# One weight tile's low half, made by VectorE alone or by VectorE and GpSimd in halves, in a hybrid decoder block

## The reference, cut to what matters

```python
h = concat(meta_tokens[16], x)                       # 272 rows of 1024
u = rms_norm(h, norm1_w)
proj = u @ w_in                                      # attention q,k,v | deltanet q,k,v | gates, beta, decay
y_a = differential_attention(a_q, a_k, a_v, ...)     # two softmax maps per head, 8 heads, blocks of 128 queries
y_d = gated_deltanet(d_q, d_k, d_v, d_gate, ...)     # causal convolution of 4 taps + SiLU, then a chunked delta rule
mixed = sigmoid(gate_a) * (y_a @ w_branch_attn) + sigmoid(gate_d) * (y_d @ w_branch_dn)
h = h + mixed @ w_out
h = h + hierarchical_moe(rms_norm(h, norm2_w), ...)  # 32 experts, top 1 group, top 2 experts in it
out = rms_norm(h, final_norm_w)[16:]
```

## Time and profile before

| what | value |
| --- | --- |
| median of 3 runs | 670.09 us (669.33 to 672.49) |
| the profiled execution | 666.38 us, of which the span from the first to the last instruction is 664.5 us |
| busy share of the span | PE 91%, PEld 76%, DVE 49%, ACT 40%, POOL 8% |
| mean granted TensorE clock | 0.969 |
| bytes read from HBM | 154 MB, 233 GB/s over the span |

### The profile page before, as it was taken

How to read it: one execution, slowest core, us unless ns; L and a number is a source line. 1 busy time by engine, 2 the same in 40 slices (tenths; PEclk the granted TensorE clock), 3 DMA queues, 4 the chain that set the end, 5 groups by cost and what they waited for, 6 DMA issues and landing times.

```text
span 664.5 us, 14325 instructions
## 1 busy us (share of the span) xinstructions
PE 603.1 (91%) x5931; PEld 505.1 (76%) x5931; DVE 327.3 (49%) x693; ACT 268.8 (40%) x598; POOL 55.2 (8%) x102
## 2 busy tenths in 40 slices
PE   8999999899987998999999999999999788687874
PEld 8999989788987888999899999997554443334451
DVE  5344376888876768465757478624112110111112
ACT  6245567676769445323532665413110010000003
POOL 8300011111000001100310120000000000000000
PEclk9799999999999999999999999999999977887999
DMA  9744543243335323221223259999999999999994
GB/s 290 237 158 161 177 141 106 86 128 127 128 127 190 124 68 128 66 66 64 65 66 114 79 174 341 419 420 419 421 364 421 419 424 421 424 421 423 419 409 160
DMA packets 68560, 156.04 MB, mean 235 GB/s; under 512 B 4818, under 2 KB 54116, under 8 KB 56596
## 3 DMA queue, kind: packets, MB, share of 16 engines
q1 hardware_dynamic: 67136, 154.89, 61.5%
q0 software_dynamic: 176, 0.17, 0.2%
q10 hardware_dynamic: 1188, 0.12, 0.2%
HBM read 154.12 MB, written 1.05 MB: 233 GB/s over the span
## 4 chain that ended last, share of the span: by engine, by line
PE 63%; DMA 10%; SPq 8%; ACT 8%; DVE 6%; issue 3%; ACTq 0%; DVEq 0%
PE bank L840 32%; DMA arena<-in_expert_w_gate_dram 8%; PE bank L1251 6%; SPq L511 6%; PE bank L1027 5%; PE bank L825 3%; SPq L606 2%; DMA arena<-in_expert_w_down_dram 2%; PE bank L1005 2%; PE bank L1232 2%; DVE ring_lo L329 1%; PE bank L1276 1%; ACT w_hi L324 1%; PE bank L1287 1%; PE bank L908 1%
## 5 line engine op out<-in xcount | busy, mean ns | idle before, releaser
L840 PE MATMUL bank<-uT_hi,w_hi 128*128 128x272 f32 (+1 forms) x568 | 169.0, 297 | 6.5 <-issue 4.9
L840 PE MATMUL bank<-uT_lo,w_hi 128*128 128x272 f32 (+1 forms) x568 | 162.9, 287 | 0.0
L840 PE MATMUL bank<-uT_hi,ring_lo 128*128 128x272 f32 (+1 forms) x568 | 162.6, 286 | 0.0
L329 DVE TENSOR_TENSOR ring_lo<-arena,w_hi 128x1024 fp32r<-128x1024 f32 x88 | 108.8, 1238 | 48.2 <-ACT w_hi L324 48.1
L840 PEld LDWEIGHTS bank<-uT_hi,w_hi 128*128 128x128 f32 x568 | 107.9, 190 | 11.5 <-issue 9.9
L840 PEld LDWEIGHTS bank<-uT_lo,w_hi 128*128 128x128 f32 x568 | 107.8, 190 | 0.5 <-issue 0.5
L840 PEld LDWEIGHTS bank<-uT_hi,ring_lo 128*128 128x128 f32 x568 | 108.0, 190 | 0.0
L324 ACT ACTIVATE w_hi<-arena 128x1024 fp32r<-128x1024 f32 x88 | 91.8, 1051 | 0.7 <-DMA arena<-in_w_in_dram 0.5
L1251 PE MATMUL bank<-arena 128*32 128x256 f32 x1024 | 64.8, 410 | 19.1 <-DMA arena<-in_expert_w_gate_dram 19.1
L1251 PEld LDWEIGHTS bank<-arena 128*32 128x32 f32 x1024 | 35.1, 118 | 43.8 <-issue 23.8
L1896 DVE SCALAR_TENSOR_TENSOR arena<-arena 128x272 f32<-128x272 f32 x72 | 35.9, 499 | 19.4 <-ACT arena L1413 18.9
(11 more groups left out here) (367 smaller groups left out, 1031.9 us busy)
## 6 DMA issues: line engine op xcount, KB each, us to landing
arena<-in_w_in_dram SPq DMA_DIRECT2D x36, 1024.0 KB, 5.0
arena<-in_expert_w_gate_dram SPq DMA_DIRECT2D x32, 1024.0 KB, 26.0
arena<-in_expert_w_up_dram SPq DMA_DIRECT2D x32, 1024.0 KB, 22.1
arena<-in_expert_w_down_dram SPq DMA_DIRECT2D x29, 1024.0 KB, 22.0
arena<-in_w_branch_attn_dram SPq DMA_DIRECT2D x4, 1024.0 KB, 5.2
arena<-in_w_branch_dn_dram SPq DMA_DIRECT2D x4, 1024.0 KB, 5.3
arena<-in_w_out_dram SPq DMA_DIRECT2D x4, 1024.0 KB, 8.5
arena<-in_expert_w_down_dram SPq DMA_DIRECT2D x6, 512.0 KB, 18.7
```

The source lines that it names most:

```text
L329: nc.vector.tensor_tensor(low_of(SPLIT[q]), src, w_hi[q % NSPLIT].bitcast(F32), ALU.subtract).then_inc(w_lo_ready, 1)
L840: last = pe.matmul(ps[:, 0:b.shape[2]], a[:, c, :], b[:, c, :], start=(c == 0 and i == 0), stop=(c == NC - 1 and i == 2))
```

## The change

In the slots the low part of a tile is made by two engines. For the tiles in `SHARED`, 24 to 47 (all of dq, dk and dv), VectorE's `split_low` now covers chunks 0 to 3 alone (128x512 in place of 128x1024), and a new function `split_low_second` has GpSimd make chunks 4 to 7, under a semaphore of its own, `w_lo_second`. TensorE waits for it as well before the tile's first matmul. GpSimd's instructions are laid out by slots for this: `att_prep` of three units first, and then in each slot the `att_prep` that is due in it (after the unit of the slot has been biased), the copy of k in slot 18, and the half of tile 24 + m + 2, for m from -2 to 21. Nothing else moves; no DMA is added, removed or moved.

```diff
--- before.py
+++ after.py
@@ -284,6 +284,7 @@
         ssq3_ready, var3_ready, rstd3_ready, out_ready = sem("ssq3_ready"), sem("var3_ready"), sem("rstd3_ready"), sem("out_ready")
         weighted, out_a = sem("weighted"), sem("out_a")
         last_in, half_sum = sem("last_in"), sem("half_sum")
+        w_lo_second = sem("w_lo_second")
 
 
         w_in_v = w_in[0].rearrange("(c p) n -> p c n", p=P)
@@ -302,9 +303,13 @@
 
 
 
+        SHARED = range(FIRST["dq"], FIRST["gate"])
+
         def wait_split(eng, q):
             eng.wait_ge(w_hi_ready, q + 1)
             eng.wait_ge(w_lo_ready, q + 1)
+            if q in SHARED:
+                eng.wait_ge(w_lo_second, q - SHARED.start + 1)
 
         def split_source(eng, q):
 
@@ -324,9 +329,16 @@
             nc.scalar.activation(w_hi[q % NSPLIT], src, ACT.Copy).then_inc(w_hi_ready, 1)
 
         def split_low(q):
-            src = split_source(nc.vector, q)
+            src, hi, lo = split_source(nc.vector, q), w_hi[q % NSPLIT], low_of(SPLIT[q])
             nc.vector.wait_ge(w_hi_ready, q + 1)
-            nc.vector.tensor_tensor(low_of(SPLIT[q]), src, w_hi[q % NSPLIT].bitcast(F32), ALU.subtract).then_inc(w_lo_ready, 1)
+            part = slice(0, NC // 2 if q in SHARED else NC)
+            nc.vector.tensor_tensor(lo[:, part], src[:, part], hi[:, part].bitcast(F32), ALU.subtract).then_inc(w_lo_ready, 1)
+
+        def split_low_second(q):
+            src, hi, lo = split_source(nc.gpsimd, q), w_hi[q % NSPLIT], low_of(SPLIT[q])
+            nc.gpsimd.wait_ge(w_hi_ready, q + 1)
+            part = slice(NC // 2, NC)
+            nc.gpsimd.tensor_tensor(lo[:, part], src[:, part], hi[:, part].bitcast(F32), ALU.subtract).then_inc(w_lo_second, 1)
 
         def splits_at(n):
 
@@ -723,10 +735,18 @@
                 pool.tensor_scalar(bias[:, b, 0:nk], dist[:, t, 0:nk], 2.0 ** (-(h + 1)) / SCALE, 0.0,
                                    ALU.mult, ALU.add).then_inc(bias_ready, 1)
 
-            for i in range(ATT_UNITS):
+            for i in range(NPREP):
                 att_prep(i)
-            pool.wait_ge(silu_ready, 2 * H)
-            pool.tensor_copy(dkT_meta, dkT[:, :, 0:META]).then_inc(k_meta, 1)
+            for m in range(FIRST_SLOT, SLOTS_A):
+                i = unit_at(m)
+                if i is not None and i + NPREP < ATT_UNITS:
+                    att_prep(i + NPREP)
+                if m == 18:
+                    pool.wait_ge(silu_ready, 2 * H)
+                    pool.tensor_copy(dkT_meta, dkT[:, :, 0:META]).then_inc(k_meta, 1)
+                for q in splits_at(FIRST["dq"] + m):
+                    if q in SHARED:
+                        split_low_second(q)
 
             def dn(t, c, s):
                 w = work[c]
```

## The result

The changed kernel takes 675.81 us in the median of 4 runs (674.80 to 676.43), the kernel before 669.71 us in the same comparison (664.80 to 672.49, 4 runs). The ratio is 1.0117, 95% interval 1.0074 to 1.0159: slower by about 1%. Two later comparisons of the same pair gave 1.0073 (1.0043 to 1.0103) and 1.0108 (1.0081 to 1.0135). All 22 runs of the changed kernel have a mean of 674.5 us, the 44 runs of the kernel before beside them 668.7: 5.8 us more. A difference "by the times" is worked out from the ratio.

The account below looks back on a forecast made before the run. In slots 6 to 17 VectorE and TensorE are nearly full, and VectorE's loop ends the waits. 5.0 + 1.2 + 0.4 + 0.3 + 0.6 = 7.5 us, on 670.09, gave 677.6 us; range 672.0 to 686.0.

Parts of the forecast that it names:

- step 1: Odd slots 1 to 17: GpSimd's half delays VectorE's run by 1.1, the split returns 0.54; 9 x 0.56 = 5.0 us.
- hold of 1.1: Time GpSimd's half keeps VectorE out: a two-SBUF-input multiplication taking 1.51 beside GpSimd, less 0.42 alone.
- Step 2: Even slots 0 to 10, VectorE: GpSimd's half makes the next first tap wait; six slots, 0.2 each, 1.2 us.
- Step 3: Even slots 0 to 10, TensorE: tile starts 1.1 later; costs after slots 4 and 8, 2 x 0.2 = 0.4 us.
- Step 4: Slots 12, 14, 16: GpSimd's half runs beside VectorE's bias instructions, which run on; 0.1 each, 0.3 us.
- Step 5: Slots -2 to -1 and 18 to 21: only slot 20 costs, its halves running one behind the other; 0.6 us.
- pair of splits at 381.19: Earlier trace: two adjacent VectorE splits took 3.43 in place of 2.35; GpSimd got in between, evidence for turns at boundaries.
- the forecast's bounds: The predicted delay with other holds: 6.6 us with a hold of 1.0, 11.2 with 1.35.
- Faster: Back-to-back VectorE runs keep GpSimd out until they pause; odd slots lose 4.9 us, result 665.2 or up to 668; chance 0.08.
- No change: Delay absorbed behind slot 17, in TensorE's wait for ScalarE or expert weights; 670 to 673, say 671; chance 0.12.
- Much slower: GpSimd's half costs 1.66: 0.56 more in each of 15 slots, 8.4 us, result 686; chance 0.10.

Follow-up runs that it names:

- odd_only: Changed kernel with GpSimd halves only for the 12 tiles split in odd slots; 671.57 us against 668.73 for the kernel before, ratio 1.0050.
- third profile: The last of three profiles taken of the unaltered changed kernel, of an execution of 671.97 us, without the clock's fall at slot 10.
- even_only: Changed kernel with GpSimd halves only for the 12 tiles split in even slots; 670.59 us against 668.73 for the kernel before, ratio 1.0050.
- half_left_out: Changed kernel with GpSimd's half not made, TensorE reading chunks 0 to 3 in its place; 665.77 us against 668.73 for the kernel before, ratio 0.9938.
- late_copy_slots: Changed kernel sharing only tiles split in slots -1, 1, 3, 7, 11, 15, 19, GpSimd waiting for VectorE's half; 666.39 us against 668.91, ratio 0.9961.
- order_only: Changed kernel's layout of GpSimd instructions by slots, but no tile shared; 668.95 us against 668.73 for the kernel before, ratio 1.0004.
- write_only: Changed kernel with VectorE making all 8 chunks and GpSimd's halves replaced by scratch memsets, still awaited by TensorE; 669.35 us against 668.44, ratio 1.0008.
- both_make: Changed kernel with VectorE making all 8 chunks and GpSimd's subtractions going to scratch, still awaited by TensorE; 677.37 us against 668.44, ratio 1.0146.
- half_first: Changed kernel with GpSimd's half put ahead of the bias preparation in each slot; 670.67 us against 668.44 for the kernel before, ratio 1.0045.
- late_ask: Changed kernel with GpSimd's half also waiting until VectorE's half of the tile is done; 671.53 us against 668.44 for the kernel before, ratio 1.0054.

## Why the prediction was right, and where its sizes were off

The prediction was +7.5 us, 677.6, slower with 0.80. Measured are 675.81 us and +4.9 to +7.8 in the three comparisons. The direction and the mechanism held. The sum is about 1.7 us too large (5.8 over all runs), and it hides two errors of opposite sign: step 1 was too large, and the clock was missing. That it lies so near is in part luck.

**Step 1, odd slots: right mechanism, 2.3 us too large.** The sum said 9 x 0.56 = 5.0; odd_only shows 2.71. GpSimd does get in at the next boundary of a back-to-back run, which was the point on which the sign hung. The hold of 1.1 taken from the delta rule was 1.0, so 0.49 a slot in place of 0.56. That is the smaller part, 0.5 us over seven slots. The larger is in the count: slot 1 gains 0.53 where it should have lost 0.56, and behind slot 16 the halves together gain 0.21 where slot 17 should have lost 0.56. In slot 1 the high part comes late in VectorE's run: GpSimd asks at 117.58, and the only boundary left, at 117.81, is the one to VectorE's own half, which goes first. GpSimd's row says 2.05 us in place of 1.27, and no tap waits. Why it lost that boundary, 0.23 us behind its request, while it got others 0.17 to 0.29 us behind (slots 15 and 7), no run here tells. In slot 17 a tap is blocked like the others (1.03 us between slots 16 and 17), but 0.76 comes back by slot 18, so the slot costs 0.27. In slot 19 nothing is blocked and the split's 0.54 is a gain, which the prediction put at nothing. I had counted nine slots by the pattern of slot 5 alone.

**Step 2, even slots on VectorE: 1.2 us said, 0.2 there.** The first tap behind the even slot's half is held up in every one of these slots, by more than was said in some: 0.69 us in slot 3, 0.58 in slots 5 and 9 (the row at 134.06), 0.90 in slots 7 and 11, in place of 0.50. But it costs the loop next to nothing. In slot 7 of the third profile the tap starts 1.72 us behind the split of slot 6 and is held up by 0.4; in odd_only it waits for ScalarE until 2.11 us behind it, and the instruction after it begins 2.65 us behind the split in both. So the pairs 6 to 8 and from 10 to 12 on are equal in the changed kernel and odd_only to 0.02. Only in slot 3 does the tap start at the same time in both, and 2 to 4 shows the 0.2.

**Step 3, the same slots on TensorE: right where it was placed.** It said 0.97 for the pairs 4 to 6 and 8 to 10 in place of what steps 1 and 2 give; the third profile has 1.03 and 1.04, and even_only, which has no odd halves, 1.05 and 1.04. So the two costs do not add up there: the longer way counts. Steps 2 and 3 together were 1.6 us by the prediction; the third profile less odd_only is 4.21 - 2.92 = 1.3.

**Step 4, slots 12, 14, 16: right, and even less.** The bias instructions, which read a bank, run on beside GpSimd's half (170.76 to 172.04), and only VectorE's half waits:

```profile
170.87 0.43 DVE L1894 CUSTOM_DVE_ANT_0 arena<-bank,arena 128x272 f32<-128x272 f32 x1
...
171.24 1.35 DVE L335 TENSOR_TENSOR ring_lo<-arena,w_hi 128x512 fp32r<-128x512 f32 x1
```

0.3 us was said; the pairs 12 to 14 and 14 to 16 are those of odd_only to 0.01.

**Step 5, slots 18 to 21: the size right, the way only in part.** 0.6 us was said; 16 to 22 is 0.39 + 0.21 = 0.60 longer than in odd_only. The prediction had TensorE follow slot 20's half. With even halves alone that is where it shows: even_only is 0.59 longer between slots 21 and 22. In the changed kernel GpSimd's half of slot 21 runs directly behind that of slot 20 and blocks the first tap of slot 21:

```profile
206.85 3.04 POOL L341 TENSOR_TENSOR ring_lo<-arena,w_hi 128x512 fp32r<-128x512 f32 x2 [2.37 <-ACT w_hi L329]
```

```profile
208.91 1.28 DVE L1916 SCALAR_TENSOR_TENSOR arena<-arena 128x272 f32<-128x272 f32 x1 [1.40 <-ACT arena L1433]
```

The distance from slot 20 to 21 is 0.76 us longer than before, and 0.07 in odd_only, where slot 21's half comes earlier. The same size by another way is luck.

**What the sum lacked: the clock.** 2.71 + 1.29 + 0.60 = 4.60 us is the third profile. A fall of the clock behind the wait of 2.2 us adds 1.5 and makes the 6.14 of the first two. The prediction had the start of the tile 1.1 us later, on top of an idle time of 1.46 us that stood in the earlier trace rows, and never added the two up or asked what TensorE's clock does after that. Two smaller slips stand in its working: the pair of splits at 381.19 is lengthened by 3.43 - 2.35 = 1.1 us, not by 1.2, and of the forecast's bounds the lower, 6.6, changes the hold in the nine slots of step 1 alone, the upper, 11.2, in fifteen slots; with fifteen in both the lower is 6.0.

**The rivals.** *Faster* asked for a VectorE run that keeps GpSimd out until it pauses. Eight odd slots, 3 to 17, deny it, each with a row of 1.39 to 1.55 us in VectorE's run; slot 1 is the one place that looks like it, and half_left_out and late_copy_slots show the gain that it would have brought (-4.0 and, with seven halves, -2.0 us in the slots). *No change* needed a place behind slot 17 that takes the delay back: 16 to 22 is longer, not shorter, and nothing behind it is. *Much slower* needed a hold of 1.66 and gets 1.0 to 1.06. That nothing would be moved at all is excluded by order_only and odd_only.

**What was to show it.** GpSimd's halves were to be 1.1 to 1.4 us unless they had to wait: the shortest take 1.26 and 1.27, and up to 1.8 where VectorE's half began a few hundredths ahead (2.05 in slot 1). One instruction of VectorE's run was to take about 1.5 us: 1.55. The first tap of odd slots was to come 0.2 later; it was longer, not later (step 2). TensorE's idle time ahead of tiles 6 and 10 was to grow by 1 us: at tile 6 it grew from nothing to 1.25, at tile 10 from 1.46 to 2.21. The stretch was to grow by 7 us: from the split of slot 1 to that of slot 19, 78.8 us before, it grew by 4.5 (third profile) to 6.1 (first). Everything behind was to keep its lengths: the profile of the kernel before is the odd one there, as order_only shows.

## What to carry to other kernels

Work moved from VectorE to GpSimd is taken out of VectorE again when, at that moment, GpSimd reads SBUF and VectorE has an instruction with two inputs from SBUF: here 1.0 us lost for 0.54 us saved. What decides is what stands beside it, so give GpSimd its share only where VectorE reads a bank or waits, and where TensorE does not wait for it, slot by slot; seven places chosen so gave 0.4%, twenty-four without a choice cost 0.9%. And where an engine on the critical path already waits, add the new delay to that wait before pricing it, since of two ways round a loop only the longer one counts, while a longer idle time of TensorE can cost its clock as well.

## What the runs showed that I had not expected

- TensorE's clock can fall behind an idle time of 2 us in the middle of a busy stretch. In the profiles there are six waits of 2.0 us or more ahead of a tile of the slots: 2.02 (even_only), 2.03 (write_only), 2.81 (both_make), 2.21, 2.23 and 2.24 (changed). Behind five of them the granted clock goes to the lower level, behind the 2.24 it doesn't. Behind single shorter ones ahead of a tile, up to 1.72 us in even_only, it stays. But 2 us is no line to rely on. Behind slot 21 TensorE waits twice, 1.59 to 1.86 us and then 1.49, with 0.4 us of matmuls between, and behind the first or the second the granted clock falls in 13 of the 14 profiles, the kernel before being the one without. In the kernel before:

```profile
214.32 0.41 PE L855 MATMUL bank<-arena 128*128 128x128 f32 x2 [1.83 <-ACT arena L1437]
...
216.22 0.36 PE L840 MATMUL bank<-uT_hi,w_hi 128*128 128x256 f32 x1 [1.49 <-issue]
```

- Who asks first decides, to a few hundredths of a us: in slot 5 GpSimd asks 0.04 ahead of the boundary and gets it, in slot 18 VectorE's half begins 0.04 ahead and GpSimd's waits. Slot 1 is the one exception seen. In half_first GpSimd asks at 130.97, 0.48 us ahead of VectorE's half, and it is VectorE's that takes 1.36 us, while GpSimd's takes its 1.29.
- An instruction of VectorE with one input from SBUF isn't always spared. The bias instructions, which read a bank and one operand from SBUF, run on beside GpSimd's half; but in late_ask a TENSOR_SCALAR of 128x272 with one tensor read from SBUF takes 1.17 us (from 103.39) in place of 0.42 beside the half that begins at 103.12.
- Whether GpSimd pays for writing fp32r isn't settled. Its half takes 1.27 us undisturbed, where a multiplication of 128x512 in fp32 has 1.35 with VectorE beside it; but both_make's subtraction, which writes fp32 and reads the high part alone, takes 1.04. It differs in its operands as well.
